# A two-block network with two mixture-of-experts layers: expert weights fetched in pairs of units, a tenth holding tile, a re-ordered feature layout, and extra matmuls in the router

## The reference, cut to what matters

```python
def ec_moe(h, w_router, w_gate, w_up, w_down):      # h: 1 x 256 x 1024, 16 experts, capacity 32
    cap = 2 * 256 // 16
    aff = softmax(h @ w_router)                     # 256 x 16
    g, idx = top_k(aff.T, cap)                      # each expert takes its 32 best rows
    xs = h[idx]                                     # 16 x 32 x 1024
    a = silu(einsum('ecd,edf->ecf', xs, w_gate)) * einsum('ecd,edf->ecf', xs, w_up)
    y = einsum('ecf,efd->ecd', a, w_down) * g[..., None]
    return zeros.at[idx].add(y)
# x = x + g_f * ec_moe(modulate(x, norm_ffn[l], sh_f, sc_f), ...)
```

## Time and profile before

| | |
|---|---|
| median of 3 runs | 1678.0 us (1674.99 to 1681.05) |
| profiled execution | 1678.73 us, of it the span of the trace 1676.9 us |
| TensorE busy, mean granted clock | 1334.8 us (80%), 0.886 of full |
| VectorE, ScalarE busy | 547.2 us, 348.4 us |
| mean memory traffic | 327 GB/s, 548.36 MB |
| mixture of experts, layer 0 and 1 | about 262 to 712 us, and 832 to 1264 us |

### The profile page before, as it was taken

The page is one execution under the profiler, slowest core; times in us unless marked ns, Lnnn a source line. Parts: engine busy times, 40 slices in busy tenths (PEclk is TensorE's granted clock), DMA queues, the critical chain, the costliest instruction groups (busy, mean ns, idle before and its releaser), DMA issues.

```text
span 1676.9 us, 29699 instructions
## 1 busy us (share of the span) xinstructions
PE 1334.8 (80%) x12432; PEld 902.8 (54%) x12432; DVE 547.2 (33%) x1175; ACT 348.4 (21%) x616; POOL 27.9 (2%) x54
## 2 busy tenths in 40 slices
PE   4899996776676675789877667667667999899999
PEld 3798583432233232389734323223234888779997
DVE  2575664111000010147531101001013674455554
ACT  2412531000000000053400000000003332344443
POOL 2020100000000000000000000000000000000000
PEclk8999997988878778799989887787778999999999
DMA  9988798999999999994799999999999541355540
GB/s 341 356 278 305 257 404 359 418 422 422 422 422 422 422 422 422 413 360 163 268 381 417 422 422 422 422 422 422 421 421 390 197 133 33 126 176 181 195 152 26
DMA packets 145646, 548.36 MB, mean 327 GB/s; under 512 B 9711, under 2 KB 77713, under 8 KB 96297
## 3 DMA queue, kind: packets, MB, share of 16 engines
q1 hardware_dynamic: 142928, 542.97, 82.5%
q10 hardware_dynamic: 1080, 3.64, 0.6%
q0 software_dynamic: 1568, 0.77, 0.4%
HBM read 546.29 MB, written 1.05 MB: 326 GB/s over the span
## 4 chain that ended last, share of the span: by engine, by line
PE 44%; DMA 43%; DVE 7%; ACT 2%; issue 2%; SPq 1%; DVEq 0%; ACTq 0%
DMA ring<-in_moe_w_up 33%; PE bank L700 8%; DMA ring<-in_moe_w_down 7%; PE bank L526 6%; PE bank L804 6%; PE bank L566 5%; PE bank L1227 5%; PE bank L827 2%; PE bank L595 2%; DMA ring<-in_ada_w 1%; DMA ring<-in_w_in 1%; DMA ring<-in_attn_w_in 1%; DVE ring_split L1548 1%; PE bank L715 1%; PE bank L1156 1%
## 5 line engine op out<-in xcount | busy, mean ns | idle before, releaser
L804 PE MATMUL bank<-ring,scratch 128*32 128x256 f32 x3840 | 302.5, 467 | 144.3 <-DMA ring<-in_moe_w_up 100.8
L804 PEld LDWEIGHTS bank<-ring,scratch 128*32 128x32 f32 x3840 | 134.4, 129 | 296.8 <-DMA ring<-in_moe_w_up 153.9
L827 PE MATMUL bank<-ring,scratch 128*32 128x256 f32 x2016 | 159.9, 469 | 49.6 <-DMA ring<-in_moe_w_down 35.5
L1504 DVE COPY scratch<-bank 128x256 f32<-128x256 f32 x32 | 13.6, 424 | 432.9 <-PE bank L813 432.9
L700 PE MATMUL bank<-scratch_split,ring_split 128*128 128x256 f32 x1248 | 151.4, 283 | 3.7 <-DVE ring_split L1548 3.7
L700 PEld LDWEIGHTS bank<-scratch_split,ring_split 128*128 128x128 f32 x1248 | 150.5, 191 | 5.3 <-DVE ring_split L1548 4.1
L827 PEld LDWEIGHTS bank<-ring,scratch 128*32 128x32 f32 x2016 | 68.2, 132 | 135.0 <-DMA ring<-in_moe_w_down 63.3
L1548 DVE TENSOR_TENSOR ring_split<-ring,ring_split 128x2048 fp32r<-128x2048 f32 x48 | 110.1, 2293 | 75.8 <-ACT ring_split L2125 75.7
L2112 ACT ACTIVATE scratch<-bank 128x256 f32<-128x256 f32 x32 | 12.3, 383 | 485.0 <-PE bank L804 485.0
L526 PE MATMUL bank<-ring,hT 128*128 128x256 f32 (+1 forms) x512 | 111.7, 377 | 1.3 <-DVE hT L1315 0.7
L2125 ACT CAST ring_split<-ring 128x2048 fp32r<-128x2048 f32 x48 | 91.4, 1906 | 57.2 <-PE bank L1227 36.7
(11 more groups left out here) (443 smaller groups left out, 1441.1 us busy)
## 6 DMA issues: line engine op xcount, KB each, us to landing
ring<-in_moe_w_down SPq DMA_DIRECT2D x126, 1024.0 KB, 26.5
ring<-in_moe_w_gate SPq DMA_DIRECT2D x120, 1024.0 KB, 24.9
ring<-in_moe_w_up SPq DMA_DIRECT2D x120, 1024.0 KB, 26.7
ring<-in_ada_w SPq DMA_DIRECT2D x48, 1024.0 KB, 9.0
ring<-in_w_ff SPq DMA_DIRECT2D x32, 1024.0 KB, 5.3
ring<-in_conv_w_in SPq DMA_DIRECT2D x12, 1024.0 KB, 12.5
ring<-in_attn_w_in SPq DMA_DIRECT2D x10, 1024.0 KB, 11.2
ring<-in_w_in SPq DMA_DIRECT2D x7, 1024.0 KB, 11.8
```

Of the source, the lines that this page charges most:

```text
L804: mm = nc.tensor.matmul(GU[32 * j:32 * j + 32, m * 256:(m + 1) * 256], xs[:, k % 2, 16 * k - k % 2 * 16:16 * k - k % 2 * 16 + 32], W[:, (k ...
L827: mm = nc.tensor.matmul(Y[32 * g:32 * g + 32, 0:256], actT[:, b, 32 * j:32 * j + 32], W[:, b * D + g * 256:b * D + (g + 1) * 256], start=( ...
```

## The change

- **Pairs.** `load_expert` now lays a matrix out in blocks of 512 rows, partition p holding rows 4p to 4p+3, 16 KB in one run. For experts 2 to 14 one transfer of 2 MB fills two neighbouring slots (an even one and the next), counted by `pair_landed[q // 2]`. Experts 0, 1 and 15 still come as single units, the halves (8 KB) of such a run.
- **Pairs wait for pairs.** SP waits until both units of the pair's place are read: expert 2's pairs for MOE_READ 4, 6, 8, 10, 12 and 24; a pair (s, s+1) of a later expert for unit s+1 of the one before.
- **Ten extra tiles.** `EXTRA` = 10, `TURN` = 2, so expert 2 begins at an even slot. The tenth is two halves of 4 KB, where `take_w` lay and in `gate`; it is fetched by two transfers after the logits. The last factor of the residual moves from `gate` to a tile of its own, `moe_gate`; `take_w` is gone, VectorE multiplies `take_p` by `aff` for each expert instead of copying.
- **Feature order.** To fit the new layout the gather streams `x[:, t, g::4]` (every fourth float), the gate and up matmuls stream two floats of each four (`expert_cols`), the transposes read contiguous columns, and gain and shift come from `rows_gain` and `rows_shift`. These are filled by 16 small matmuls and 4 vector instructions for each layer, at the end of `pe_ada_cols(l, 1)` and `ada_cols(l, 1)`; one more small load (GpSimd's queue), four more transposes and one copy serve them at the start.
- **Router.** `keep_clock(n)` issues n matmuls of 128x512 into bank 3, whose result nobody reads: 2 before the wait for `aff_ready`, 5 before `order_ready`, 1 before `take_ready`.
- TensorE's loop over experts runs 2 to 14; expert 15 is written out.

```diff
-        take_p, take_w = carve(S, 16, TT, NEXP, CAP), carve(S, 20, TT, NEXP, CAP)
+        take_p = carve(S, 16, TT, NEXP, CAP)
+        two_halves = (carve(S, 20, D), carve(GT, 0, D))
...
+                T = tile(pe, f"adaQ{l}")
+                for q in range(2):
+                    for a in range(4):
+                        at = 16 * q + 4 * a
+                        for half in (0, 64):
+                            mm = nc.tensor.matmul(T[half:half + 64, at:at + 4], ada_rows[l][(3 + q) // 2][:, (3 + q) % 2, a::4],
+                                                  ident[:, 0::32], start=True, stop=True)
+                done(f"adaQ{l}", mm)
...
+            pe.wait_ge(free[3], turns[3])
+            def keep_clock(n):
+                for _ in range(n):
+                    nc.tensor.matmul(banks[3][:, :], ident, x[:, 0, 0:512], start=True, stop=True)
+            keep_clock(2)
             sig("aff_ready").take(pe)
...
+            keep_clock(5)
             sig("order_ready").take(pe)
...
+            keep_clock(1)
             sig("take_ready").take(pe)
...
                         mm = nc.tensor.matmul(banks[2][32 * g:32 * g + 32, 0:256], own,
-                                              x[:, t, g * 256:(g + 1) * 256], start=(t == 0), stop=(t == 1))
+                                              x[:, t, g::4], start=(t == 0), stop=(t == 1))
...
-                                GU[32 * j:32 * j + 32, m * 256:(m + 1) * 256], xs[:, k % 2, 16 * k - k % 2 * 16:16 * k - k % 2 * 16 + 32],
-                                W[:, (k % 2) * D + j * 256:(k % 2) * D + (j + 1) * 256],
+                                GU[32 * j:32 * j + 32, m * 256:(m + 1) * 256].rearrange("q (p b) -> q p b", b=2),
+                                xs[:, k // 4, 32 * (k % 4):32 * (k % 4) + 32],
+                                expert_cols(W[k % 2], j),
...
+        def expert_cols(W, j):
+            return W[:, 512 * (j // 2):512 * (j // 2) + 512].rearrange("q (p h b) -> q p h b", h=2, b=2)[:, :, j % 2, :]
...
-                        ins = V.tensor_copy(w_rep[:, :, j, :], take_w[:, :, e, :])
+                        ins = V.tensor_tensor(w_rep[:, :, j, :], take_p[:, :, e, :],
+                                              bc(aff[:, :, e].unsqueeze(2), [P, TT, CAP]), ALU.mult)
...
+                if isinstance(e, int) and e in (0, 1, NEXP - 1):
+                    sp.dma_start(tile_, rows[:, half]).then_inc(there_sem, 16)
+                else:
+                    q = seats[seat[f"moe{l}"] + (s + TURN) % SLOTS][0]
+                    sp.dma_start(ring[:, q:q + 2, :].rearrange("p s n -> p (s n)"), rows).then_inc(there_sem, 16)
...
+                    for s in range(0, SLOTS, 2):
+                        sp.wait_ge(MOE_READ, 12 * e0 + (TURN + s + 2 if s < EXTRA else 14 + s))
+                        load_expert(l, 2, s)
+                    with sp.Fori(3, NEXP - 1) as e:
+                        for s in range(0, SLOTS, 2):
+                            sp.wait_ge(MOE_READ, e * 12 + (12 * (e0 - 1) + s + 2))
+                            load_expert(l, e, s)
                     for s in range(SLOTS):
-                        sp.wait_ge(MOE_READ, 12 * e0 + (TURN + s + 1 if s < EXTRA else 13 + s))
-                        load_expert(l, 2, s)
-                    with sp.Fori(3, NEXP) as e:
-                        for s in range(SLOTS):
-
-                            sp.wait_ge(MOE_READ, e * 12 + (12 * (e0 - 1) + s + 1))
-                            load_expert(l, e, s)
+                        sp.wait_ge(MOE_READ, 12 * (e0 + NEXP - 2) + s + 1)
+                        load_expert(l, NEXP - 1, s)
...
-EXTRA = 9
+EXTRA = 10
```

More of the change, by code:

```diff
@@ L348, in build @@
         extra_landed = [sem(f"extra_landed{i}") for i in range(EXTRA)]
+        pair_landed = [sem(f"pair_landed{i}") for i in range(SLOTS // 2)]
         unit_read = sem("unit_read")
@@ L844, in pe_moe @@
             expert(1)
-            with pe.Fori(2, NEXP) as e:
+            with pe.Fori(2, NEXP - 1) as e:
                 expert(e)
+            expert(NEXP - 1)
         def pe_turn_rows_after(pe, name, src=None, paired=False):
@@ L872, in _ @@
                     pe_turn_rows_after(pe, "nx")
-            pe.wait_ge(loads["rows"], 16 * (len(ROWS) + 1))
+            pe.wait_ge(loads["rows"], 16 * (len(ROWS) + 2))
             T = tile(pe, "vec")
@@ L877, in _ @@
                 mm = nc.tensor.transpose(T[:, P + 8 * a:P + 8 * a + 8], ffn_rows[:, a::2], ident[0:8, 0:8])
+            for a in range(4):
+                mm = nc.tensor.transpose(T[:, P + 16 + 4 * a:P + 20 + 4 * a], ffn_rows4[:, a::4], ident[0:4, 0:4])
             done("vec", mm)
@@ L2100, in moe @@
                 T = product(s, f"gate{l}.5")
-                empty(s, f"gate{l}.5", A.copy(gate[:, 0:256], T[:, 0:256]))
+                empty(s, f"gate{l}.5", A.copy(moe_gate[:, :], T[:, 0:256]))
                 load_table(ACT.Silu)
@@ L2498, in load_expert @@
                 mat = w[("moe_w_gate", "moe_w_up", "moe_w_down")[s // 4]][l]
[L2499 to L2500 removed]
+                r0, half = (s % 4 - s % 2) * 256, slice((s % 2) * UNIT, (s % 2 + 1) * UNIT)
+                rows = mat[e, r0:r0 + 512, :] if isinstance(e, int) else mat[e][r0:r0 + 512, :]
+                rows = rows.rearrange("(p a) n -> p (a n)", a=4)
                 dst, there_sem, _ = expert_unit(l, e, s)
[L2502 removed]
+                if dst is two_halves:
+                    for a in range(2):
+                        sp.dma_start(dst[a], rows[:, half][:, a * D:(a + 1) * D]).then_inc(there_sem, 16)
+                    return
+                tile_ = extra[l][s] if isinstance(e, int) and e == 1 and s < EXTRA else \
+                    ring[:, seats[seat[f"moe{l}"] + (s if isinstance(e, int) and e == 0 else (s + TURN) % SLOTS)][0], :]
+                if isinstance(e, int) and e in (0, 1, NEXP - 1):
[3 more added lines that the diff above has]
+                    sp.dma_start(ring[:, q:q + 2, :].rearrange("p s n -> p (s n)"), rows).then_inc(there_sem, 16)
             for item in units:
```

57 lines of the change are left out of this document (36 added, 21 removed).

## The result

The changed kernel takes **1682.9 us** (median of 20 executions, 1677.7 to 1691.1) against 1678.9 us for the kernel before in the same comparison. The ratio is 1.0029 with a 95% interval of 1.0016 to 1.0041: slower by 3 to 7 us. The forecast was 1666.5 us and "faster". The profiled execution spans 1679.9 us, 3.0 more than that of before.

What follows compares the result with a forecast made beforehand. Each layer's experts were taken as bound by TensorE at the start, then by transfer rate. Packets -10.9, the start -2.8 and small matmuls +1.5 gave -12.2 us on 1678.73: 1666.5 us, 8-in-10 range 1660 to 1683.

Steps and rivals of the forecast that it cites:

- the clock: Router's waits: eight extra matmuls hold full clock into expert 0, saving 3.6 us a layer, less 0.5 delay in layer 0.
- the packets: Long transfer-bound part of the experts: 16 KB packets run at 428.5 GB/s instead of 422, saving 10.9 us.
- the holes: Start of layer 0's experts: the dry queue at 279 to 283 fills, one of about 2 us appears at 316 to 318.
- the tenth tile: Ahead of the experts: one more unit fills most of the hole, but by itself gives nothing, its time spent waiting at 316.
- The pair's wait: Start of each layer's experts: expert 3's first pair needs two units read, not one, costing 0.9 us more.
- Rival 3: Router: the clock is not held, or extra matmuls at half clock delay the order; 1675 us, chance 0.12.
- the gather: Gather streaming every fourth float: half the +0.87 us bound, 0.43, three times before expert 2 reads, +1.3 us a layer.
- Gate and up: Experts' gate and up matmuls streaming two floats of four: taken to cost nothing, zero us.
- Rival 1: Experts' gate and up stream at two thirds of the rate, 10.7 instead of 7.15 us; kernel slower, 1685 us, chance 0.2.
- The small matmuls: Feature order's 16 matmuls a layer, on TensorE's chain ahead of layer 0's experts: +1.5 us, bounds 0.5 and 3.5.

Runs made afterwards that it cites:

- e9: Kernel of e7 with every 2 MB transfer made as two of 1 MB at the same waits: 1686.4 us, ratio 1.0044 to before.
- e4: Changed kernel with expert 2 fetched in single units, each as soon as its slot is read: 1681.2 us, ratio 1.0021 to before.
- e11: Kernel of e7 with expert 2 fetched in single units, each as soon as its slot is read: 1672.6 us, ratio 0.9973 to before.
- e1: Kernel before with only the change's four new tiles declared at the change's places, never used: 1685.9 us, ratio 1.0050 to before.
- e2: Changed kernel with its four new tiles declared behind all others: 1677.0 us, ratio 0.9996 to before.
- e5: Kernel of e1 with 64 bytes more, so older tiles move by 256 or 1280 bytes: 1676.8 us, ratio 0.9993 to before.
- e13: Kernel before with only the eight keep_clock matmuls added at the change's three places: 1678.1 us, ratio 1.0001 to before.
- e3: Changed kernel without the eight keep_clock matmuls: 1682.2 us, ratio 1.0021 to before.
- e10: Kernel of e7 without the eight keep_clock matmuls: 1679.3 us, ratio 1.0010 to before.
- e7: Kernel of e2 with the gather streaming two floats of each four instead of one: 1673.9 us, ratio 0.9981 to before.
- e15: Kernel of e11 with the two adaQ products in banks of their own, so later products keep their old banks: 1671.1 us, ratio 0.9954 to before.
- e14: Kernel before with TensorE's loop ending at expert 14 and expert 15 written out: 1680.1 us, ratio 1.0011 to before.
- e12: Kernel of e7 with layer 0's 16 small matmuls put two steps later: 1677.9 us, ratio 0.9987 to before.
- e8: Kernel of e2 with layer 0's 16 small matmuls put two steps later: 1679.1 us, ratio 1.0006 to before.

## Why the prediction was wrong

Faster by 12.2 us was forecast, and the kernel is 4.9 us slower. Two steps failed by more than the times' noise: untouched code was priced at nothing while its tiles moved, and the clock's 7.2 us did not come.

**Right: the packets.** -10.9 us was forecast from a line through three sizes; 428 GB/s were forecast and measured, and e9 gives 10.6 us.

**Half right: the holes.** The hole at 279 to 283 is filled, and the tenth tile's time is spent waiting later on, as foreseen. The chain also had the right owner in the start, TensorE. The hole foreseen at 316 to 318, ahead of expert 3's first pair, is the one at 320 to 325, 3.0 us and not 2: expert 2's matmuls begin at 319.82, forecast 314.7. The one at 314 to 317 was not foreseen: the pair of places 10 and 11 was to follow closely on the queue's end at 310.9, and is issued at 314.05, since expert 1 ends later than forecast. The pair's wait was counted at 0.9 us in the start of each layer; e4 and e11 say 1.3 us for both together, within what they resolve.

**Failed first: the addresses had no step at all.** The prediction costed what the change computes and where it puts it, and took the price of all untouched code as zero. e1 shows 8 us for four declarations, e2 5.5 us in the changed kernel, and e5 that the loss goes when the distance is 256 or 1280 bytes. That alone brings the forecast from 1666.5 to 1672. No row of before shows it, since every row has the same addresses; but the diff does show tiles declared ahead of others.

**Failed second, and the largest miss: the clock, -7.2 us.** The step read the fall of the clock at 263 and its return at 283.5 as one event that the router's waits cause and eight matmuls undo. The long spell is indeed ended by them (1.00 at the first expert, as forecast). Two parts of the step failed. One is that the clock then stays up: in e13 it fell again inside expert 0 in both layers, and half of the 3.6 us was gone. The other is the delay, taken as 0.5 us in layer 0 and 0 in layer 1: it is nothing in layer 0 and 1.8 us in layer 1, above its bound of 1.2, as the first two matmuls run there at half clock. Together the trace leaves 1.7 us of 7.2, and the times none (1.0001). In the changed kernel with its doubled gather the term is empty as well (e3), since there the clock is back before the first expert without them. Only beside the cheap gather do the matmuls return 5 us (e10 against e7). Rival 3 had this as "not held", 1675 us, and gave it 0.12.

**Failed third: the gather, +2.6 us.** Taken at half of its upper bound; the trace has the whole of it, 1.99 against 1.07 us, 0.9 us at each of three experts in two layers, 5.5 us. The times give 2.5 us for it (e7 against e2), good to 3. Between two ends with a row for each, the middle was taken without a row that spoke for it. The Trainium skill, SBUF — State Buffer, section Door 1, says that a 16-byte line needs two hits for the full rate; with the gather at its upper bound that made 1669 in place of 1666.5. Here the trace agrees with it: 1.99 and 1.11 us. Its other half, that two of four keep the full rate, is nearly so: gate and up take 7.5 us and not 7.15, 5% more.

**Gate and up, 0 us.** Rival 1's factor of 1.5 did not come: the factor is 1.05 (7.52 for 7.15). That is 0.37 us for an expert and, for experts 0 and 1 and the first pair of 2 in both layers, some 1.6 us. The sign turned, but not by this rival's mechanism.

**The small matmuls, +1.5 us.** 2.09 us in the trace, inside the bounds of 0.5 and 3.5; the router begins 2.5 us later on the mean. The 1.79 us of waiting behind them, which were counted as cover in part, are still there behind them (1.62).

**Not seen: the banks, 0 us.** Two more products in the turn of eight banks make a wait of 2.1 us at the other end of the kernel; that the kernel is shorter without it is not shown (e15). Nor was a price thought of for writing expert 15 out (e14).

The sum from what was measured: -10.6 (packets) + 5.5 (addresses) + 2.5 (gather) + 2.5 (small matmuls) + 2.1 (banks) + 1.6 (gate and up) + 1.3 (pair wait) + 0 (clock) = +4.9 us, against 1.0029 x 1678.9 - 1678.9 = +4.9. Only the packets and the addresses are well clear of the noise. Each other term is good to 1 to 3 us, the one for the banks is the length of a wait, and e14's 1.8 us are left out, so that they meet so well is luck. The range ended at 1683 and held the median, but by rival 1's account, which was wrong; the true one had no place in it, since all that was varied lay in the code that the diff names.

## What to carry to other kernels

A diff that declares a tile ahead of others, or takes one more turn in a rotation of buffers, changes every later place: cost it, or declare new tiles last and give new products buffers of their own (the first is shown here, the second only as a wait that goes). Price an access pattern at the end that a like row supports, and let the gather and the main stream share the cheap one (two neighbours of four, not one). A clock held through a wait is worth its price only if it then stays up: look for the short falls elsewhere in the trace before counting on it.

## What the runs showed of the hardware

- **Addresses.** Matmuls of 512 columns whose loaded operand lies in `scratch` and whose streamed one in the ring take 395 ns for 392 or 393 when `scratch` begins at a multiple of 256 bytes and not 64 beyond one (five kernels against twelve), and whole kernels differ by 5.5 to 8 us with the places of tiles alone (e1 against before, after against e2); moving all by 256 and 1280 bytes costs nothing (e5).
- **Strides.** A gather (16 matmul records of 256 columns) whose moving operand is every fourth float takes 1.99 us where contiguous data take 1.07, and with two neighbours of four 1.11. A stationary operand with every second float loads in 207 ns, a contiguous one in 146 (the same transposes behind the gather, in e7 and in the changed kernel).
- **Packets.** 16 KB packets run at 428 GB/s, 8 KB at 422, in the same kernel (e7, e9).
- **Clock.** Spells of about 3 us at half clock stand in the traces at changing places while TensorE is busy: at 317 to 320 in before, in expert 0 in e11, e12, e13 and e15 and in layer 1 of e7, at expert 1 in e8. No run shows what sets their places.
